# First mixer's units rotated by four, and its gate products packed by row halves

## The reference

```python
h = _rmsnorm(x, norm_mix)
xr, gr, q, k, v, ga, gb = jnp.split(h @ w_in, splits, axis=-1)      # each 1024 wide

xc = _centred_dwconv(xr, conv_w, conv_b)                            # 4 taps
h_fwd = _rglru_scan(xc, ...)                                        # and h_bwd on the flipped input
y_lru = (h_fwd + h_bwd) * jax.nn.gelu(gr)

q = _rmsnorm(q.reshape(B_, S, N_HEADS, HEAD_DIM), q_norm) * (HEAD_DIM ** -0.5)
k = _rmsnorm(k.reshape(B_, S, N_HEADS, HEAD_DIM), k_norm)
y_att = _neighbourhood_attention(q, k, v, rpb)

y = jax.nn.sigmoid(ga) * y_lru + jax.nn.sigmoid(gb) * y_att
x = x + y @ w_out
```

## Time and profile before

| | |
|---|---|
| runs | 2439.14, 2436.75, 2438.6 us; median 2438.6 |
| the profiled execution | 2440.55 us, its span 2438.4 us |
| mean granted TensorE clock | 0.986 |
| TensorE busy | 2360.7 us, 97% |
| VectorE, ScalarE, POOL busy | 1299.3, 994.9, 176.7 us |
| the chain that ended last | TensorE 87%, ScalarE 5%, VectorE 4%, issue 4% |
| first mixer | about 376 to 828 us of the span |

### The profile page before, as it was taken

The page is one execution under the profiler, slowest core; times in us unless marked ns, Lnnn a source line. Parts: engine busy times, 40 slices in busy tenths (PEclk is TensorE's granted clock), DMA queues, the critical chain, the costliest instruction groups (busy, mean ns, idle before and its releaser), DMA issues.

```text
span 2438.4 us, 30936 instructions
## 1 busy us (share of the span) xinstructions
PE 2360.7 (97%) x10918; PEld 1899.4 (78%) x10918; DVE 1299.3 (53%) x1832; ACT 994.9 (41%) x1481; POOL 176.7 (7%) x140
## 2 busy tenths in 40 slices
PE   8999999999999799999999989999989998999998
PEld 6888887777776588888877768888877766888887
DVE  5443436556666544443365566555248986655524
ACT  4223223676666532222234444333234454433322
POOL 0000002333554000000000000000000000000000
PEclk9999999999999899999999989999999999999999
DMA  4333322222223132233232222223313222232321
GB/s 162 97 100 102 102 90 84 86 88 97 89 73 99 38 101 95 95 111 104 70 102 83 86 69 84 97 96 109 100 47 104 70 70 69 78 103 95 117 95 47
DMA packets 62183, 219.91 MB, mean 90 GB/s; under 512 B 7664, under 2 KB 12272, under 8 KB 62112
## 3 DMA queue, kind: packets, MB, share of 16 engines
q1 hardware_dynamic: 60944, 216.86, 26.9%
q10 hardware_dynamic: 1168, 2.12, 0.3%
HBM read 216.83 MB, written 2.12 MB: 90 GB/s over the span
## 4 chain that ended last, share of the span: by engine, by line
PE 87%; ACT 5%; DVE 4%; issue 4%; ACTq 0%; DMA 0%; DVEq 0%; SPq 0%
PE bank L1867 27%; PE bank L1869 26%; PE bank L1868 26%; ACT m_prob L235 1%; PE bank L546 1%; DVE wL L1860 1%; ACT wH L1855 1%; PE bank L536 1%; PE bank L978 0%; PE bank L1006 0%; PE bank L988 0%; PE bank L1566 0%; PE bank L2239 0%; PE bank L2238 0%; PE bank L2237 0%
## 5 line engine op out<-in xcount | busy, mean ns | idle before, releaser
L1867 PE MATMUL bank<-H,wH 128*128 128x512 f32 x3012 | 1193.2, 396 | 34.9 <-DVE L L1941 15.4
L1869 PE MATMUL bank<-H,wL 128*128 128x512 f32 x3012 | 1176.9, 391 | 0.0
L1868 PE MATMUL bank<-L,wH 128*128 128x512 f32 x3012 | 1176.2, 390 | 0.0
L1860 DVE TENSOR_TENSOR wL<-raw,wH 128x1024 fp32r<-128x1024 f32 (+1 forms) x361 | 475.9, 1325 | 615.5 <-ACT wH L1855 615.5
L1867 PEld LDWEIGHTS bank<-H,wH 128*128 128x128 f32 x3012 | 567.9, 189 | 165.2 <-issue 22.4
L1869 PEld LDWEIGHTS bank<-H,wL 128*128 128x128 f32 x3012 | 567.8, 189 | 120.5
L1868 PEld LDWEIGHTS bank<-L,wH 128*128 128x128 f32 x3012 | 568.4, 189 | 118.7 <-issue 3.8
L1855 ACT ACTIVATE wH<-raw 128x1024 fp32r<-128x1024 f32 (+1 forms) x361 | 396.0, 1105 | 225.4 <-PE bank L1869 204.5
L2059 ACT ACTIVATE H<-prod 128x512 f32 (+1 forms) x88 | 55.7, 632 | 243.5 <-DVE prod L2124 243.5
L2104 DVE TENSOR_TENSOR gate_s<-bank,rstd 128x512 f32<-128x512 f32 x88 | 60.8, 691 | 113.7 <-PE bank L1869 110.7
L641 POOL TENSOR_TENSOR m_bias<-m_run,m_mask 128x256 f32<-128x256 f32 x64 | 75.8, 1221 | 408.1 <-DMA m_run<-in_rpb 408.1
(11 more groups left out here) (267 smaller groups left out, 1696.4 us busy)
## 6 DMA issues: line engine op xcount, KB each, us to landing
raw<-in_w_ffn_gu SPq DMA_DIRECT2D x88, 512.0 KB, 3.4
raw<-in_w_in SPq DMA_DIRECT2D x56, 512.0 KB, 3.9
raw<-in_w_ffn_down SPq DMA_DIRECT2D x32, 704.0 KB, 4.0
raw<-in_w_up_2a SPq DMA_DIRECT2D x44, 512.0 KB, 3.4
raw<-in_w_up_2b SPq DMA_DIRECT2D x44, 512.0 KB, 3.4
raw<-in_w_in_even SPq DMA_DIRECT2D x24, 512.0 KB, 4.4
raw<-in_w_in_odd SPq DMA_DIRECT2D x24, 512.0 KB, 3.4
raw<-in_w_down_2a SPq DMA_DIRECT2D x16, 704.0 KB, 4.3
```

The costliest lines, as they stand in the source:

```text
L1860: dve.tensor_tensor(w_l, raw_at(st, j), w_h.bitcast(F32), ALU.subtract).then_inc(S.lo_done, 1)
L1867: pe.matmul(out, w_h, xh[:, k0 + k], start=start and k == ks[0], stop=False)
L1868: pe.matmul(out, w_h, xl[:, k0 + k], start=False, stop=False)
L1869: last = pe.matmul(out, w_l, xh[:, k0 + k], start=False, stop=stop and k == ks[-1])
```

## The change

Three things are changed together.

The order of the units: IN1's columns are laid out as xr, q, k, v, gr, ga, gb (`MIX1_ORDER`), and a body's seven slots now hold units 4, 5, 6 of its own tile (gr, ga, gb) and units 0 to 3 (xr, q, k, v) of the next. Ahead of body 0 stand only the first four units of tile 0; the last body has three units of its own and then the starts of w_out's products.

The gate products: `gate_w` holds, for each direction, one 128 x 128 tile instead of two. Its rows 0 to 63 carry the first LRU block's r and i side by side, its rows 64 to 127 the second block's i and r. A direction is then one product over the rows 0 to 63 into bank 4 and one over the rows 64 to 127 into bank 5. ScalarE applies the Tanh to four halves of 64 partitions instead of two full tiles; TensorE's second pair waits for all four.

What goes with it: `early` has seven tiles of y, `late` one; the gelu's square and Tanh, the copy of y and the evacuations change their slots; the convolution of tile 0 is done in the start-up; the parameters' transfers stand behind unit 4 in SyncE's order, and for tile 0 no longer wait for the normalised tiles.

```diff
     def sp(sp):
-        for j in range(PER):
+        for j in range(5):
             k.load_unit(sp, st, 0, j)
-        sp.wait_ge(S.v_ready, site.v0 + DT)
+        sp.wait_ge(S.u_ready, site.u0 + DT)
         sp.dma_start(mask[:], t["win_mask"]).then_inc(M.mask_loaded, 16)
         load_params(sp, 0)
+        for j in range(5, PER):
+            k.load_unit(sp, st, 0, j)
...
         with sp.Fori(2, N) as u:
             for j in range(PER):
                 k.load_unit(sp, st, u, j)
-            load_params(sp, u)
+                if j == 4:
+                    load_params(sp, u)
...
     def act_gates(act, p, d):
 
-        for g, dst in ((0, t2), (1, ti)):
-            act.wait_ge(M.gates, 4 * p + (2 * d + g + 1))
-            wait(act, M.lru, 6 * p + (3 * d - 3))
-            n = (2 * d + g) * 8
-            act.activation(dst[:, d], bank[4 + g][:], ACT.Tanh, scale=0.5, bias=k.colat(k.hbg, n, p))\
-               .then_inc(M.gate_act, 1)
-        act.wait_ge(M.gate_act, 8 * p + (4 * d + 1))
+        lower, upper = slice(0, 64), slice(64, P)
+        wait(act, M.lru, 6 * p + (3 * d - 3))
+        for half, r_rows, i_rows in ((0, lower, upper), (1, upper, lower)):
+            act.wait_ge(M.gates, 4 * p + (2 * d + half + 1))
+            rows = (lower, upper)[half]
+            for g, dst, src in ((0, t2, r_rows), (1, ti, i_rows)):
+                act.activation(dst[rows, d], bank[4 + half][src, :], ACT.Tanh, scale=0.5,
+                               bias=rows_at(k.hbg, rows, (2 * d + g) * 8, p)).then_inc(M.gate_act, 1)
+        act.wait_ge(M.gate_act, 12 * p + (6 * d + 3))
...
+    def unit_at(p, n):
+
+        return (p, n + 4) if n < 3 else (p + 1, n - 3)
+
...
             slot(0)
             if tail:
                 act_probT(act, p - 1, 2)
-            if prev:
-                evac(act, p, 5)
-                for n in range(2):
-                    wait(act, M.lru, 6 * p)
-                    act.wait_ge(M.evac, PER * p + (3 + n))
-                    act.activation(sqk[:, n], qk[:, n], ACT.Square).then_inc(M.sqk, 1)
-                wait(act, M.y1, 2 * p)
-                act.activation(g2[:], gr[:], ACT.Square).then_inc(M.g2, 1)
+            evac(act, p, 2)
+            for n in range(2):
+                wait(act, M.lru, 6 * p)
+                act.wait_ge(M.evac, PER * p + (2 + n))
+                act.activation(sqk[:, n], qk[:, n], ACT.Square).then_inc(M.sqk, 1)
             slot(1)
             if tail:
                 act_probT(act, p - 1, 3)
-            if prev:
-                evac(act, p, 6)
-                act.wait_ge(M.g2p, 2 * p + 2)
-                act.activation(g2[:], g2[:], ACT.Tanh, scale=GELU_C).then_inc(M.gth, 1)
+            evac(act, p, 3)
             slot(2)
-            if units:
-                evac(act, u, 0)
-            slot(3)
-            if units:
-                evac(act, u, 1)
+            evac(act, p, 4)
+            act.wait_ge(M.evac, PER * p + 5)
+            wait(act, M.y1, 2 * p)
+            act.activation(g2[:], gr[:], ACT.Square).then_inc(M.g2, 1)
             if tail:
                 act.wait_ge(M.y_f, p)
                 act.activation(k.tile_of(k.H, site.y + p - 1), y[:], ACT.Copy).then_inc(M.y_hi, 1)
...
+            slot(3)
+            evac(act, p, 5)
...
             slot(4)
...
+            act_gates(act, p, 1)
+            evac(act, p, 6)
+            act.wait_ge(M.g2p, 2 * p + 2)
+            act.activation(g2[:], g2[:], ACT.Tanh, scale=GELU_C).then_inc(M.gth, 1)
+            wait(act, M.hsum, p)
...
         dve_scaled(dve, 0)
         dve_scaled(dve, 1)
         k.split_lo(dve, st, 0, 4)
+        dve_conv(dve, 0)
         k.normal_dve(dve, site, 0, 3)
...
-    early = (0, 1, 2, 3, 4, 5)
+    early = (0, 1, 2, 3, 4, 5, 6)
...
     def pe_gates(pe, p, d):
-        for g in range(2):
-            if d == 1:
-                pe.wait_ge(M.gate_act, 8 * p + (g + 1))
-            pe.matmul(bank[4 + g][:], gate_w[:, 2 * d + g], xc[:], start=True, stop=True).then_inc(M.gates, 1)
+        if d == 1:
+            pe.wait_ge(M.gate_act, 12 * p + 4)
+        for half, rows in enumerate((slice(0, 64), slice(64, P))):
+            pe.matmul(bank[4 + half][:], gate_w[rows, d], xc[rows, :], start=True, stop=True).then_inc(M.gates, 1)
...
         pe.wait_ge(S.consts, 48)
-        body(-1, True, False, False)
-        body(0, True, True, False)
+        k.first_products(pe, c, site, [bank[b][:] for b in FIRST_BANK[:2]])
+        dense(0, 2)
+        dense(0, 3)
+        body(0, True, False)
...
+MIX1_ORDER = np.arange(7 * D).reshape(7, D)[[0, 2, 3, 4, 1, 5, 6]].reshape(-1)
```

More of the change, by code:

```diff
@@ L256, in act_gates, with body, slot @@
         act.activation(t2[:, d], t2[:, d], ACT.Tanh, scale=sc, bias=sc).then_inc(M.gate_act, 1)
+    def unit_at(p, n):
+        return (p, n + 4) if n < 3 else (p + 1, n - 3)
     def act(act, after):
-        def body(p, units, prev, tail):
+        def body(p, units, tail):
             u = p + 1
[L262 to L266, removed]
+            def slot(n):
+                i, j = unit_at(p, n)
+                if n < 3 or units:
+                    if not (isinstance(i, int) and i == 0):
+                        k.split_hi(act, st, i, j)
+                elif n - 3 < after.early:
+                    k.split_hi(act, after, 0, n - 3)
             slot(0)
@@ L313, in body @@
-            if units:
-                evac(act, u, 2)
+            slot(3)
+            evac(act, p, 5)
+            for n in range(2):
+                act.wait_ge(M.qk_stat, 2 * p + (n + 1))
+                act.activation(qkr[:, n], bank[6 + n][:], ACT.Ln, bias=k.eps_col[:]).then_inc(M.qk_rs, 1)
+            for n in range(2):
+                act.wait_ge(M.qk_rs, 4 * p + (n + 1))
+                act.activation(qkr[:, n], qkr[:, n], ACT.Exp, scale=-0.5).then_inc(M.qk_rs, 1)
+            act_gates(act, p, 0)
@@ L410, in dve_scaled @@
         src, by = bank[FIRST_BANK[j]][:], k.rstd_mix[:]
-        if j == 4:
+        if j == 3:
             dve.tensor_tensor(perm(vT[:]), rows_of(src), rows_of(by), ALU.mult).then_inc(M.evac, 1)
             return
-        dst = (xr[:, 2:2 + SEQ], gr[:], qk[:, 0], qk[:, 1], None, tha[:], thb[:])[j]
+        dst = (xr[:, 2:2 + SEQ], qk[:, 0], qk[:, 1], None, gr[:], tha[:], thb[:])[j]
         dve.tensor_tensor(dst, src, by, ALU.mult).then_inc(M.evac if j < 5 else M.scaled0, 1)
-    def dve(dve, after):
[L418 to L425, removed]
-            slot(0)
[L427 to L438, removed]
-                                             ALU.add).then_inc(M.conv, 1)
@@ new lines, in dve, with body, slot @@
+    def dve(dve, after):
+        def body(p, units, tail):
+            first = isinstance(p, int) and p == 0
+            def slot(n):
+                i, j = unit_at(p, n)
+                if n < 3 or units:
+                    if not (isinstance(i, int) and i == 0):
+                        k.split_lo(dve, st, i, j)
+                elif n - 3 < after.early:
+                    k.split_lo(dve, after, 0, n - 3)
+            slot(0)
+            if not first:
+                dve_conv(dve, p)
@@ L440, in body @@
             slot(1)
[L441 to L442 removed]
+            if first:
+                dve_scaled(dve, 4)
             slot(2)
@@ L603, in body @@
-            unit(3)
-            if prev:
-                pe_score_pair(pe, p, 0)
-                pe.wait_ge(M.v_ev, 2 * p + 1)
-                for n in range(3):
-                    last = pe.transpose(bank[6][:, P * n:P * n + P], vT[:, 64 + P * n:64 + P * n + P], k.ident[:])
-                last.then_inc(M.v_tr, 1)
+            for n in range(2):
+                pe.wait_ge(M.sqk, 2 * p + (n + 1))
+                if n == 0:
+                    wait(pe, M.p_ev, 4 * p)
+                else:
+                    wait(pe, M.yatt_used, p)
+                pe.matmul(bank[6 + n][:], k.heads1[:], sqk[:, n], start=True, stop=True).then_inc(M.qk_stat, 1)
@@ new lines, in body @@
+            unit(2)
+            pe_gates(pe, p, 1)
+            pe.wait_ge(M.evac, PER * p + 4)
+            pe.wait_ge(M.qk_rs, 4 * p + 1)
+            for n in range(4):
+                last = pe.transpose(bank[6][:, P * n:P * n + P], vT[:, P * n:P * n + P], k.ident[:])
+            last.then_inc(M.v_tr, 1)
+            unit(3)
+            pe_score_pair(pe, p, 0)
+            pe.wait_ge(M.v_ev, 2 * p + 1)
+            for n in range(3):
+                last = pe.transpose(bank[6][:, P * n:P * n + P], vT[:, 64 + P * n:64 + P * n + P], k.ident[:])
```

242 lines of the change are left out of this document (110 added, 132 removed).

## The result

The changed kernel takes 2453.96 us (median of 4 runs, 2451.86 to 2456.83) against 2438.66: a ratio of 1.0067, 95% interval 1.0054 to 1.0079. It is slower, by 15.3 us (0.7%). The forecast was 2439.6, its range ended at 2450. The profiled execution took 2453.2 us with a span of 2451.4, 13.0 longer than the one before.

What follows compares the result with a forecast made beforehand. Bound by the ScalarE and VectorE chain from S to U. Start -18.7, body 0 +1.3 and +3.2, bodies 1 to 6 +15.4, gate pairs -4.3, end +4.3 and -0.15: +1.0, 2441.6 profiled, forecast 2439.6 us; range 2428 to 2450.

Steps and rivals of the forecast that it cites:

- the size of the half-height Tanh: Gate Tanh on ScalarE: 0.57 us for each of four with 64 rows, 2.28 us more per body; lower bound half.
- the chain from S to U: From q/k statistic product (S) to first dense unit (U): sets the body, 37.07 us, growing by 2.57 to 39.64.
- The rival that partly came true: the clock: TensorE's clock falls behind the 2.0 us wait at the v transposes in every body: 2447 to 2459 us, chance 19%.
- TensorE's waits: In a middle body: 0.95 us at the second gate pair, 2.0 at the v transposes, 0.6 at U, all hidden.
- The saving ahead of S: Gate pair ahead of the q/k statistic product, packed by row halves: 1.06 us instead of 1.72, saving 0.66.
- The copy of y: On ScalarE, moved ahead of the q/k statistic product where there is room: 0.62 us off the chain.
- the split of slot 5: VectorE's split, 1.23 us undisturbed, meets POOL's later operations ahead of the exponential: 0.37 us more, bounds 0 and 0.8.
- the prediction's three terms: Reordering on the chain of a body: copy of y -0.62, gelu Tanh +0.54, POOL beside VectorE's split +0.37 us.
- half the time: Rival at the gate Tanh: those of 64 rows take half, -9.1 us, 2430.5 us; chance 13%.
- pauses on ScalarE: Rival: added ScalarE work falls into pauses, bodies are TensorE's 49.9 us, seven times 3.6 shorter, 2414 us; chance 10%.
- no overlap of the row halves: Rival at the packed gate products: the row halves don't run together, +4.3 us, 2443.9 us; chance 10%.
- The end: Last body and tail of the first mixer: 40.5 us before, 44.8 after, +4.3, less 0.15 for w_out's early tile.

Runs made afterwards that it cites:

- run 2: The kernel before with only the gate products packed by row halves (the row halves alone): 2459.81 us, ratio 1.0082.
- run 3: The new unit order with full-array gate products, each gate Tanh cut into two of 64 rows on the same partitions: 2459.94 us, ratio 1.0084 to the kernel before.
- run 4: The new unit order with full-array gate products, each gate Tanh cut into two by columns (128x256): 2434.23 us, ratio 0.9982 to the kernel before.
- The rotation alone: The changed kernel's unit order without the packing, full-array gate products and two Tanh of 128 rows: 2429.64 us, ratio 0.9953 to the kernel before.
- run 6: The new unit order with full-array gate products, gelu Tanh moved behind the first four exponentials: 2446.14 us, ratio 1.0021 to the kernel before.
- run 9: The new unit order with full-array gate products, only POOL's last gelu and gate products held until after four exponentials: 2445.68 us, ratio 1.0021 to the kernel before.

## Why the prediction was wrong, point by point

**The failed step: the size of the half-height Tanh.** The prediction took 0.57 us for each, "what one of 128 rows takes from its neighbour's start to its own", and let it range downwards only. It is 0.71, in runs 2 and 3 as in the change: 3.36 us per body instead of 2.28, +1.08 in each of 8 bodies, 8.6 us. The duration of 0.67 stood in the earlier trace rows and would have been a bound on the other side; that the overlap of 0.1 could be lost was not considered. The whole miss in a middle body lies on the chain from S to U (40.47 us instead of 39.64), none from U to S (13.77 instead of 13.80). The Trainium skill, ScalarE: Activation LUTs, What ACT_TABLE_LOAD costs, gave an estimate of 0.61 with its 93 ns of overlap; without the overlap its figures give an estimate of 0.71, which is the pitch in the trace, and for 256 columns an estimate of 0.40 with it, where run 4 shows 0.36.

**The rival that partly came true: the clock.** The prediction tied it to the wait at the v transposes, in every body, and said that it decides from a loss of 0.6 us per body. With the later copy of v that wait is 2.45, not 2.0. In four of the six middle bodies the clock falls behind it (0.79 in the window from 700, 1.00 in that from 646), and these take 54.84 to 55.08 us, the two others 54.24 and 54.31: 0.6 to 0.8 each, 2.7 in all. The wait itself is the same in all six (2.42 to 2.45). It counts once more in a later stage. The same wait as before, 2.90 us, has the clock at 1.00 behind it in the kernel before and at 0.58 in the changed one. The timelines of TensorE there, first before, then after:

```profile
2019.81 0.50 PE L1867 MATMUL bank<-H,wH 128*128 128x512 f32 x1 [2.90 <-DVE L L1522]
```

```profile
2030.22 0.80 PE L1869 MATMUL bank<-H,wH 128*128 128x512 f32 x1 [2.90 <-DVE L L1524]
```

and the windows behind them:

```profile
2019.80:2026.80 7.00, 6.65 (x27) 4.86 (x28) 2.68 (x4) 3.93 (x6) 0.00 (x0) 1.00 0.00 0
```

```profile
2030.20:2037.20 7.00, 6.98 (x19) 5.51 (x20) 2.67 (x4) 3.94 (x6) 0.00 (x0) 0.58 0.00 0
```

The rotation alone has 0.57 there too; the row halves alone and run 3 wait 2.92 and 2.90 and show full-speed products (0.50 us). From this product to the end of the span are 418.6 us before, 418.5 in the row halves alone and in run 3, and 421.2 in the changed kernel and in the rotation alone: 2.6 us go that way. The prediction had nothing for stages behind the mixer. What decides between 1.00 and 0.58 behind an equal wait was not tried and stays open; runs 4 and 6, which have the rotation too, have no spell there.

**What held.** The chain sets the body, and where the clock stays high TensorE's waits are hidden behind it: forecast 0.95, 2.0 and 0.6, measured 1.23, 2.45 and 0.48 (the Tanh term is large enough for the growth of the first two). The first gate product came at 398.92, near the 401 of the forecast. The gate pair takes 1.06 on the chain, as taken from the earlier trace rows; one line of the chain of waits:

```profile
620.84 1.06 PE bank L556 x4
```

The saving ahead of S is 0.75 to 0.76 instead of 0.66. The copy of y gives 0.60 of 0.62. POOL lengthens the split of slot 5 by 0.12 (1.35 against 1.23), not 0.37. The rotation alone changes a body by 0.03, where the prediction's three terms give 0.29. The rivals "half the time" (0.71, not 0.29), "pauses on ScalarE" (run 2: 2.69 more in a body) and "no overlap of the row halves" (1.06, not 1.72) are refuted.

**The sum again,** against the forecast of +1.0 by the step behind the mixer. By the prediction's terms the statistic product of the second body comes 14.9 us earlier than before; it came 15.6 earlier (463.50 against 479.10): -0.7. Two errors nearly cancel in that number, which is luck: ScalarE's chain in body 0 lies as if its S were 409.3 (the exponential at 431.77 less 22.48) instead of 410.8, 1.5 us better, and it has the Tanh's excess too. Six middle bodies without low clock are 54.27 instead of 53.44: +5.0. Low clock in them: +2.7. The end is 5.7 longer than before (from the last body's S at 791.84 to the next step 53.0 us, against 47.3), not 4.3 less 0.15: +1.6, two thirds of it the Tanh's 1.08. Together -0.7 + 5.0 + 2.7 + 1.6 = +8.6, and with the forecast's +1.0 the 9.6 that were measured. The stages behind add 3.4, most of it the clock at 2030. That makes 13.0, the difference of the spans; the medians differ by 15.3, 2.3 more: the profiled execution of the kernel before was 1.9 us above its median, and that of the changed one 0.8 below.

A sharper range would have asked of the Tanh what it asked of the other unknowns, a bound on either side. With the full duration of 0.67 us for each of the four the sum goes up by 8 x 0.80 = 6.4 to +7.4, about 2446 us. With the measured 2.82 us for four it goes to +9.6, about 2448, and with the clock's share (2.7 and 2.6) to 2453.

## What to carry to other kernels

Packing by array rows moved cost here from TensorE to the engine that reads the banks: count the reader's instructions before the products, and price a half-height ScalarE instruction at the full duration, without the overlap where its neighbour starts at other partitions (0.71 us here). Whether an order that keeps neighbours on the same partitions gets the overlap back is worth a run; none was made. A body can be a relay: here ScalarE up to the weight half, VectorE behind it, so an edit pays only if it is on the leg that it leaves and harms nothing on the leg that it joins, POOL's followers included. Where two edits come in one change, run each alone: here one gained some 11 us and the other lost 19; the rotation without the packing is the best version found (2428.5 to 2429.6 us, 0.5% under the kernel before). A spell of low clock has no fixed price either: 0 in the middle bodies of the row halves alone, where TensorE had a later wait to lose it in, 0.6 to 0.8 us in those of the changed kernel.

## What the runs showed of the hardware that was not expected

A ScalarE instruction of 64 partitions and 512 columns lasts 0.67 to 0.69 us like one of 128. Where it starts at another partition than its neighbour (0 or 64), in source or target, it doesn't start before that neighbour has ended (pitch 0.71 against 0.57, and the 128-row instruction behind the four the same). Where it starts at partition 0 behind a full-height neighbour, it overlaps it by 0.09 to 0.10 us, in all sixteen places of the changed kernel; in run 3, where the last bank read had started at partition 64, it didn't at eight of sixteen. One of 128 partitions and 256 columns keeps the overlap (pitch 0.36). That the start partition and not the half height decides is read from these rows and was not tried by a run of its own; why the overlap goes is not shown.

POOL working on SBUF stretches a VectorE instruction beside it by 0.4 us and more: the earlier trace rows had 0.40, and here 0.68 us became 1.10, 0.69 became 1.17 (mean of six), and one scan beside two POOL operations went from 1.22 to 2.18 (1.37 on the mean of run 9). The Trainium skill, GPSIMD Engine Reference, Specifications, has the interfaces shared with VectorE instructions of two SBUF inputs; these three have two, and the traces agree.
